# Eleven small SBUF tensors allocated earlier in a two-layer decoder kernel: the same instructions at other addresses

## The reference

```python
h = rmsnorm(x, mix_norm_g[l])
a_b, a_c, a_x, s_u, s_v, q, k, v, gates = split_cols(h @ w_in[l])   # 1024 x 7168
ya = a_b * conv3(a_c * a_x)                        # short causal convolution, 512 channels
yb = gelu(s_u) * (tril(W_s) @ layernorm(gelu(s_v)) + b)   # chunks of 128, 4 groups
yc = stick_breaking(rmsnorm(q), rmsnorm(k), v)     # 8 heads of 64, strictly causal
merged = sum_i sigmoid(gates_i + b_gate_i) * (y_i @ w_branch_out[l, i])
x = x + merged @ w_o[l]
h2 = rmsnorm(x, ffn_norm_g[l])
g, u = split(h2 @ w_gate_up[l])                    # 1024 x 5632
x = x + (silu(g) * u) @ w_down[l]                  # 2816 x 1024
```

## Time and profile before

| | |
|---|---|
| median of three runs | 1735.19 us |
| lowest and highest run | 1734.69 us, 1736.7 us |
| the profiled execution's own time | 1736.7 us |
| span of its trace, first to last instruction | 1735.0 us |
| TensorE matmul busy | 1707.1 us, 98% of the span |
| VectorE busy | 983.5 us, 57% |
| ScalarE busy | 753.3 us, 43% |
| GpSimd busy | 247.8 us, 14% |
| mean granted TensorE clock | 0.992 |

### The profile page before, as it was taken

How to read it: one execution, slowest core, us unless ns; L and a number is a source line. 1 busy time by engine, 2 the same in 40 slices (tenths; PEclk the granted TensorE clock), 3 DMA queues, 4 the chain that set the end, 5 groups by cost and what they waited for, 6 DMA issues and landing times.

```text
span 1735.0 us, 22652 instructions
## 1 busy us (share of the span) xinstructions
PE 1707.1 (98%) x7651; PEld 1403.0 (81%) x7651; DVE 983.5 (57%) x1181; ACT 753.3 (43%) x1050; POOL 247.8 (14%) x221
## 2 busy tenths in 40 slices
PE   6999999999999999999999999999999999999997
PEld 5788888888888888888877888888888888888886
DVE  5677775645565434434658867665455644444347
ACT  5466766533334223223346776754333432232233
POOL 5233140000040000000222233110002200000004
PEclk9999999999999999999999999999999999999999
DMA  5322222233333333333333222222333333333334
GB/s 157 87 73 85 61 86 84 75 96 102 103 97 92 99 93 96 97 95 98 118 114 96 71 76 85 66 86 85 97 103 97 97 97 97 97 97 97 97 97 133
DMA packets 310544, 163.84 MB, mean 94 GB/s; under 512 B 5472, under 2 KB 306648, under 8 KB 310488
## 3 DMA queue, kind: packets, MB, share of 16 engines
q1 hardware_dynamic: 308184, 158.94, 31.2%
q10 hardware_dynamic: 2304, 4.20, 0.6%
HBM read 156.83 MB, written 2.10 MB: 92 GB/s over the span
## 4 chain that ended last, share of the span: by engine, by line
PE 91%; DVEq 2%; DVE 2%; ACT 2%; POOLq 1%; issue 1%; ACTq 0%; POOL 0%; DMA 0%; SPq 0%
PE bank L507 27%; PE bank L508 27%; PE bank L511 27%; PE z L579 2%; DVEq L1494 2%; PE z L553 1%; PE z L552 1%; PE z L508 1%; PE z L511 1%; PE z L507 1%; PE z L557 1%; ACT xg_hi L797 1%; POOLq L423 1%; DVE w_lo L1115 1%; POOLq L418 1%
## 5 line engine op out<-in xcount | busy, mean ns | idle before, releaser
L507 PE MATMUL bank<-xg_hi,w_hi 128*128 128x512 f32 x1600 | 633.5, 396 | 3.4 <-ACT w_hi L779 1.7
L508 PE MATMUL bank<-xg_lo,w_hi 128*128 128x512 f32 x1600 | 627.2, 392 | 0.0
L779 ACT ACTIVATE w_hi<-raw 128x1024 fp32r<-128x1024 f32 (+1 forms) x299 | 309.3, 1036 | 538.0 <-DMA raw<-in_w_gate_up 219.3
L1115 DVE TENSOR_TENSOR w_lo<-raw,w_hi 128x1024 fp32r<-128x1024 f32 (+1 forms) x299 | 404.8, 1356 | 39.2 <-ACT w_hi L779 22.3
L511 PE MATMUL bank<-xg_hi,w_lo 128*128 128x512 f32 x1600 | 396.0, 389 | 1.5 <-DVE w_lo L1115 1.5
L507 PEld LDWEIGHTS bank<-xg_hi,w_hi 128*128 128x128 f32 x1600 | 303.4, 190 | 68.1 <-DVE xg_lo L1201 1.9
L508 PEld LDWEIGHTS bank<-xg_lo,w_hi 128*128 128x128 f32 x1600 | 303.3, 190 | 63.1 <-issue 1.2
L511 PEld LDWEIGHTS bank<-xg_hi,w_lo 128*128 128x128 f32 x1600 | 300.3, 188 | 64.1 <-DVE w_lo L1115 1.9
L1120 DVE TENSOR_TENSOR S<-bank,rstd 128x512 f32<-128x512 f32 x152 | 104.9, 690 | 264.4 <-PE bank L511 263.8
L507 PE MATMUL bank<-mid_hi,w_hi 128*128 128x512 f32 x480 | 187.0, 390 | 0.0
L508 PE MATMUL bank<-mid_lo,w_hi 128*128 128x512 f32 x480 | 186.7, 389 | 0.0
(11 more groups left out here) (191 smaller groups left out, 1678.3 us busy)
## 6 DMA issues: line engine op xcount, KB each, us to landing
raw<-in_w_in SPq DMA_DIRECT2D x112, 512.0 KB, 3.7
raw<-in_w_gate_up SPq DMA_DIRECT2D x88, 512.0 KB, 3.8
raw<-in_w_down SPq DMA_DIRECT2D x48, 512.0 KB, 3.6
raw<-in_w_o SPq DMA_DIRECT2D x19, 512.0 KB, 3.5
raw<-in_w_branch_out SPq DMA_DIRECT2D x16, 512.0 KB, 3.6
raw<-in_w_branch_out SPq DMA_DIRECT2D x16, 256.0 KB, 2.6
gates<-in_x SPq DMA_DIRECT2D x4, 512.0 KB, 5.7
mix_hi<-yb_hi ACTq DMA_DIRECT2D x8, 256.0 KB, 2.3
```

Source lines behind the costliest of these rows:

```text
L507: mm(dst[:, :], wh[:, k0 + k, :], his[k], start=(k % per == 0), stop=False)
L508: mm(dst[:, :], wh[:, k0 + k, :], los[k], start=False, stop=False)
L779: af(w_hi[at.slot(c)][:, 0:kc, :], raw[at.slot(c)][:, 0:kc, :], ACT.Copy).then_inc(hi_done, 1)
L1115: tt(w[:, 0:kc, :], r[:, 0:kc, :], h[:, 0:kc, :].bitcast(F32), ALU.subtract).then_inc(lo_done, 1)
```

## The change

Eleven calls of `sb` move up. The tiles `eps`, `par`, `gain0` and the six small ones of the layer norm (`ln_stats` to `ln_rstd`) now come behind `sw_lo`, and `conv_in` comes behind `KT`; the two names that are views (`N2`, `sq_sum` and `sq_one`) move with it.

```diff
         sw_lo = sb("sw_lo", [P, KC, P], F32R)
+        eps = sb("eps", [P, 1])
+        par = sb("par", [P, 64])
+        gain0 = sb("gain0", [P, KD])
+        ln_stats = sb("ln_stats", [P, NT, 6])
+        ln_mv = sb("ln_mv", [P, NT, 2])
+        ln_v = sb("ln_v", [P, NT])
+        ln_r = sb("ln_r", [P, NT])
+        ln_t = sb("ln_t", [P, NT])
+        ln_rstd = sb("ln_rstd", [P, NT])
         ya_hi = sb("ya_hi", [P, KC, T], F32R)
...
         KT = sb("KT", [P, T])
+        conv_in = sb("conv_in", [P, 2 + T])
         N0 = sb("N0", [P, T])
         N1 = sb("N1", [P, T])
+        N2 = conv_in[:, 2:2 + T]
+        sq_sum, sq_one = S2[:, :], N1[:, :]
 
         over = plan[0]
...
         plan[0] = max(plan[0], over + 16 * 4 * T)
-
-        conv_in = sb("conv_in", [P, 2 + T])
-        N2 = conv_in[:, 2:2 + T]
-        sq_sum, sq_one = S2[:, :], N1[:, :]
-        eps = sb("eps", [P, 1])
...
-        ln_rstd = sb("ln_rstd", [P, NT])
         assert plan[0] <= nc.sbuf_usable_end, plan[0]
```

## The result

| | before | after |
|---|---|---|
| median of five runs | 1735.19 us | 1745.35 us |
| lowest run | 1734.04 us | 1742.17 us |
| ratio (95% interval) | | 1.0061 (1.0045 to 1.0077) |
| span of the profiled execution | 1735.0 us | 1745.0 us |

The changed kernel is 0.6% slower, and the prediction of no change (1735.2 us, range 1732 to 1740) was wrong. One of the five runs of the changed kernel took 4247.25 us, for a reason that the record doesn't show; it is not in the ratio, and the median of the other 17 runs on record is 1746.32 us.

What follows compares the result with a forecast made beforehand. The prediction took TensorE's matmuls, 98% of the span, to bound the kernel. All terms were 0, leaving the profiled execution at 1736.7 us; it forecast the median unchanged at 1735.2 us, range 1732 to 1740.

Steps and rivals of the forecast that it cites:

- the fourth part's term for TensorE: Moving operands now 32 bytes past a multiple of 64, on `mid` and in attention: 0 taken, at most 13.4 us.
- Rival (1): TensorE pays for a half piece in `w_o`, `w_down` units and attention: up to 13.4 us, 1748.6 us; chance 6%.
- The second part of the prediction: Tiles whose address shifts by 576 bytes, a multiple of 64: 0 for all engines.
- the weights, `xg` and the splits at 0: Tiles that don't move, used by matmuls on `xg`, all weight loads and splits: same cost, 0.
- the small operands at 0: `eps`, `par` and the layer norm's tiles: 0 taken, under 1 us even without idle ScalarE as cover.
- GpSimd at 0: GpSimd's operations on the moved `N1`: 0 taken, at most 3 us in all, below 0.2%.
- the DMAs at 0: Load of `x`, spatial gating slabs and output: 0 taken, 0.2 us as upper bound on either side.
- Rivals (2): GpSimd's operations on `N1` 0.8 us longer each, first sum of squares 11.5 us longer: 1746.7 us; chance 3%.
- (3): GpSimd and VectorE no longer collide in the first sum of squares: 4.0 us faster, 1731.2 us; chance 3%.
- Rival (4): A stretch at the lower clock is added or taken away: 2 to 5 us either way; chance 3%.

Runs made afterwards that it cites:

- the last experiment: Changed kernel with 192 bytes left free ahead of `ya_hi` and 224 ahead of `N0`: 1734.80 us, ratio 0.999 to the kernel before.
- the two slowest kernels: Kernel before with `xg` 160 and `mid` 192 bytes later: 1776.47 us; with `xg` 96 and `mid_lo`, `mid_hi` 4 bytes later: 1775.54 us.

## Why the prediction was wrong

The step that failed is the fourth part's term for TensorE. Its bounds were 0 and 7.1 ns a matmul, and I took 0; measured are 6.7 ns on `mid`, so 9.6 us where the sum had 0. Rival (1), given 6%, happened in place and sign. Its 1748.6 us were too high by 3.2 us: it had 10.2 us for `mid` where 9.6 were measured, 3.2 for the attention where there were 1.0, nothing for `merge` where there were 1.6, and it didn't count that TensorE would wait less at the layers' ends. That its price for one matmul, 7.1 ns, comes so near the 6.7 measured is luck, since its mechanism was another (below).

Two readings led to the 0. The first was the pair of `xg` and `mid` at the same 5.44 us. I took it to show that an address doesn't matter. But their starts differ by 1024 bytes, a multiple of 256, so they are the same case twice, and no row of the kernel before had a second one. The second was VectorE's and ScalarE's indifference to starts 4 and 8 bytes off. That reading was right for them, as the rows after show, and for GpSimd. It says nothing of TensorE, whose weight loads run beside its matmuls, 81% of the span beside 98%.

The mechanism of rival (1), a row that starts within a 64-byte piece and needs one more, was wrong too, although its price nearly fits. It would have made 64 and 128 bytes free, and the start of the weights of no account; the runs show a cost at both, and 1766.76 us for the weights alone. The second part of the prediction failed for the same reason: tiles moved by 576, "a multiple of 64", were put at 0 and cost 0.10 us in each of 16 rounds of `merge`. And of the attention's 448 matmuls, which it counted whole, the scores and the values had both operands moved by the same 2656 bytes, so their distance stayed 0; only for the cumulative sums, whose weights `neg_tri` and `neg_ones` stayed, did it change.

The 16-byte lines of the Trainium skill's page "SBUF — State Buffer", section "Door 1: The DMA port swizzle", which the prediction weighed, don't explain it either: 32 bytes are two whole lines and cost 6.7 ns. The same page of the Trainium skill says in the section "Who interferes with whom" that TensorE has two independent read ports, one for the moving operand and one for the weights, and never waits on anyone. By that rule, the distance between the two reads should not matter; the measured 5.44 and 5.60 us a unit at distances of 0 and 32 speak against it.

The other steps held: the weights, `xg` and the splits at 0, the small operands at 0 (the last experiment leaves them at the new place and has no loss), GpSimd at 0, the DMAs at 0 (the load of `x` took 5.4 us from issue to landing where it had taken 5.7). Rivals (2) and (3) didn't happen. Rival (4) did, both ways: the stretches at a lower clock made one head 1.4 us longer and another 1.5 us shorter.

That the weights' read and the moving read meet somewhere in SBUF is my explanation of the table, and isn't shown; the runs show only that the distance of the two starts counts, and that the pace takes some nine matmuls to recover. Why 64 is cheaper than 32, why 4 bytes cost most, and which weight load it is (the matmul's own or the next one's, which overlaps it in the timeline), stay open.

## What to carry to other kernels

When TensorE is the bound, the addresses of its operands are part of the kernel: an edit that only allocates a small tile earlier can cost 3% of the pace of every matmul on the tiles behind it. For fp32r matmuls of 128x128 weights against 512 columns, the only ones measured in a steady stretch, keep weights and moving operands at the same start modulo 256 bytes, and fill up with free bytes behind small tiles. With a helper that rounds to 32 bytes this costs at most 224 bytes of a partition a time. When a trace is to show that something doesn't matter, check that it holds two different cases of it.

## What the runs showed of the hardware that was not expected

- The pace of a 512-column fp32r matmul depends on the distance of its two operands' starts: 226.7 ns at 0, 229 at 64 and up to 236 at 4 bytes, steady over whole stretches of the kernel.
- The slower pace carries over: behind a unit at a distance of 160, matmuls at distance 0 took 231.6 ns on the mean for nine matmuls, and 226.3 behind those.
- The spread of one kernel's runs follows the mean granted clock: 1742.17 us at 0.995 and 1751.52 us at 0.989 are the two ends of the changed kernel's 17 runs. 0.006 x 1745 is 10.5 us, and the ends lie 9.4 us apart. The kernel before spreads as much over all its runs, 1732.16 us at 0.993 to 1741.15 us at 0.989.
- A slower pace can come with a higher mean clock, but need not: 0.995 and 0.996 in the four runs with the weights moved, against 0.990 to 0.995 in the 13 of the kernel before beside them; 0.992 and 0.991 at 1776.47 and 1775.54 us, the two slowest kernels.
